# The long units of the second attention of an encoder layer: scores with keys on the partitions

## The reference

```python
def chunk_causal_attention(q, k, v):          # q, k: (B, H, S, 96), v: (B, H, S, 64)
    scale = dk ** -0.5
    for qb in range(S // 128):
        q0 = qb * 128
        L = q0 + 128
        s = einsum('bhqd,bhkd->bhqk', q[:, :, q0:L], k[:, :, :L]) * scale
        s = where(key // 64 <= query // 64, s, -inf)
        p = softmax(s)
        outs.append(einsum('bhqk,bhkd->bhqd', p, v[:, :, :L]))
```

## Time and profile before

| what | value |
|---|---|
| median of 3 runs | 1380.7 us (1379.72 to 1380.89) |
| the profiled execution | 1381.86 us, of which its span 1380.1 us |
| granted TensorE clock, mean | 0.991 |
| TensorE (PE) busy | 1321.9 us, 96% of the span |
| VectorE (DVE) busy | 834.0 us, 60% |
| ScalarE (ACT) busy | 740.3 us, 54% |
| GpSimd (POOL) busy | 161.2 us, 12% |

### The profile page before, as it was taken

The page is one execution under the profiler, slowest core; times in us unless marked ns, Lnnn a source line. Parts: engine busy times, 40 slices in busy tenths (PEclk is TensorE's granted clock), DMA queues, the critical chain, the costliest instruction groups (busy, mean ns, idle before and its releaser), DMA issues.

```text
span 1380.1 us, 21741 instructions
## 1 busy us (share of the span) xinstructions
PE 1321.9 (96%) x8200; PEld 993.1 (72%) x8200; DVE 834.0 (60%) x1639; ACT 740.3 (54%) x1422; POOL 161.2 (12%) x263
## 2 busy tenths in 40 slices
PE   6999999999999989999999999999989999999995
PEld 5888998844445744545887887888667878888884
DVE  5523125547667877675777433435746787787876
ACT  6421177456657766666334334333325677776765
POOL 1000000012240050000000000000035122221221
PEclk9999999999999999999999999999999999999998
DMA  6141113450000030102113010000667999999993
GB/s 239 22 172 46 66 62 122 183 201 17 1 1 1 2 122 22 40 32 92 46 46 138 19 43 31 31 31 31 239 232 222 328 356 340 343 345 332 360 340 108
DMA packets 89219, 186.47 MB, mean 135 GB/s; under 512 B 14094, under 2 KB 25266, under 8 KB 88370
## 3 DMA queue, kind: packets, MB, share of 16 engines
q1 hardware_dynamic: 80050, 166.11, 33.5%
q0 software_dynamic: 7008, 19.28, 5.7%
q10 hardware_dynamic: 2080, 0.01, 0.1%
HBM read 165.45 MB, written 25.56 MB: 138 GB/s over the span
## 4 chain that ended last, share of the span: by engine, by line
PE 83%; DVE 5%; ACT 4%; DMA 4%; issue 2%; POOL 1%; DVEq 0%; ACTq 0%; SPq 0%; POOLq 0%
PE psum L2504 31%; PE psum L2752 19%; PE psum L2647 7%; PE psum L2488 7%; PE psum L2670 5%; PE psum L2629 4%; PE psum L2481 4%; DMA up_stage<-in_w_up 3%; PE psum L2977 3%; PE psum L2986 1%; PE psum L2908 1%; DVE up_rest L1997 1%; PE psum L2964 1%; ACT arena L1448 1%; DVE arena L1874 0%
## 5 line engine op out<-in xcount | busy, mean ns | idle before, releaser
L1138 ACT ACTIVATE arena<-psum 128x512 f32<-128x512 f32 (+3 forms) x195 | 85.9, 494 | 84.9 <-PE psum L2670 47.4
L2647 PE MATMUL psum<-arena 64*128 64x512 f32 (+7 forms) x384 | 115.4, 519 | 8.3 <-ACT arena L1429 5.8
L1874 DVE TENSOR_TENSOR_SCAN arena<-arena,singles 128x768 f32<-128x768 f32 (+7 forms) x64 | 86.4, 1364 | 53.7 <-POOL arena L935 47.5
L2647 PEld LDWEIGHTS psum<-arena 64*128 64x128 f32 (+1 forms) x384 | 49.2, 190 | 75.6 <-issue 48.3
L2670 PEld LDWEIGHTS psum<-ident,arena 128*128 128x128 f32 x576 | 66.2, 144 | 51.6 <-ACT arena L1138 26.4
L2488 PE MATMUL psum<-arena 128*128 128x512 f32 (+2 forms) x280 | 93.8, 488 | 0.8 <-DVE arena L1855 0.8
L2670 PE MATMUL psum<-ident,arena 128*128 128x128 f32 x576 | 86.1, 287 | 8.4 <-DVE arena L1874 4.4
L2481 PE MATMUL psum<-ident,arena 128*128 128x128 f32 (+1 forms) x520 | 73.4, 278 | 17.8 <-ACT arena L1156 9.4
L1997 DVE TENSOR_TENSOR down_rest<-down_stage,down_high 128x1024 fp32r<-128x1024 f32 x60 | 71.4, 1220 | 26.8 <-ACT down_high L1471 26.8
L2481 PEld LDWEIGHTS psum<-ident,arena 128*128 128x128 f32 (+1 forms) x520 | 59.2, 139 | 33.8 <-issue 19.1
L2629 PE MATMUL psum<-arena 128*64 128x512 f32 (+3 forms) x384 | 83.4, 515 | 0.0
(11 more groups left out here) (565 smaller groups left out, 3395.9 us busy)
## 6 DMA issues: line engine op xcount, KB each, us to landing
gate_stage<-in_w_gate SPq DMA_DIRECT2D x16, 2048.0 KB
up_stage<-in_w_up SPq DMA_DIRECT2D x16, 2048.0 KB
down_stage<-in_w_down SPq DMA_DIRECT2D x15, 2048.0 KB
arena<-in_x SPq DMA_DIRECT2D x16, 512.0 KB, 3.9
arena<-in_w_mkv SPq DMA_DIRECT2D x8, 1024.0 KB, 6.2
arena<-in_w_in SPq DMA_DIRECT2D x4, 1024.0 KB, 10.9
arena<-in_w_mo SPq DMA_DIRECT2D x4, 1024.0 KB, 6.4
mv_times_w_mo_spill<-arena SPq DMA_DIRECT2D x8, 512.0 KB, 3.1
```

What stands on the lines that cost most here:

```text
L1138: do(act.activation(dst, src, ACT.Copy), s_te["act"])
L1874: do(dve.tensor_tensor_scan(w_row(u, r, a)[:, 0:L][:, ::-1], f_sb[:, n % FAILS, 0:L][:, ::-1], tiny.to_broadcast([P, L]), 1.0, ALU.mult, A ...
L2647: mm = pe.matmul(scores_of(kind, n)[:, at:end], lhs, rhs(at, end), start=True, stop=True)
```

## The change

The short units stay as they are. For a long unit:

- **Maximum pass.** ScalarE copies keys and queries of the next pair to float32r (`long_high`, 4 copies) and VectorE makes the rests (`long_rests`, 4 subtractions; for unit 4 GpSimd makes them). TensorE makes each row once, high by high only, in two products of half the row's width (`row_product`), always into banks 2 and 3. VectorE masks and takes the maximum (`row_maximum`). Row k waits for the maximum of row k - 1.
- **Shift inside the product.** The negative maxima are turned (`minus_maxima_turned`, 4 turns) and copied by ScalarE as rows 96 to 99 under the queries (`minus_maxima_copied`, 2 copies); the keys get matching rows of ones (`head_pick`). The product then gives score minus maximum.
- **Turned scores.** TensorE makes the scores again with keys on the partitions, block of 128 keys j by block, for both heads: two products each of the rests (`rest_products`) and one with the shift (`high_products`). ScalarE makes the exponentials of a block of both heads at once into `probs` (4 buffers), and writes zeros where the mask cuts (j of 4 and more). TensorE multiplies by the values (`value_products`).
- **Sums.** GpSimd adds the 8 blocks (7 additions of up to 2 x 512 columns a partition), TensorE sums over keys with a product of ones (`sums_over_keys`, bank 3), VectorE takes the reciprocal of 512 columns and multiplies (`long_out`).
- **Order.** The rows of unit u + 1 stand on TensorE at blocks 3 to 6 of unit u, two each; the first waits for `long_out(u - 1)`. The rows of unit 4 stand in unit 3, two at each block. Both late tiles are turned up in unit 1. The folded copies of the output projection's weights and the loads of the next weights wait for the new products.

```diff
+def of_block(i):
+    return PAIRS + i // ROWS, i % ROWS, P * max(0, i % ROWS - GRP)
+def added_through(i):
+    return (ROWS - 1) * (i // ROWS) + i % ROWS
...
-    return (("kf", "qf")[j], T - 2 if u == 1 else T - 1) if u in (1, PAIRS - 1) and j in (0, 1) else None
+    return (("kf", "qf")[j % 2], T - 2 + j // 2) if u == 1 else None
...
+        k_high = [over(f"mla_keys_high_{i}", F32R, at, 2, SEQ) for i, at in enumerate((36864, 41216))]
+        q_high = [[over(f"mla_queries_high_{i}{a}", F32R, at, GRP * P)[:, :] for a, at in enumerate(ats)]
+                  for i, ats in enumerate(((38912, 40704), (43264, 43776)))]
+        probs = [cut(44288 + 2 * GRP * P * i, 2, GRP * P) for i in range(4)]
+        prob_sums = [cut(at, 2, GRP * P) for at in (39424, 48384)]
+        one_over = cut(49408, GRP * P)
+        minus_max = over("minus_maxima", F32R, 16192, QK + 4 * GRP)[:, :]
+        maxima_of = cut(16304, 2 * GRP)
+        head_pick = cut(16312, 2)
+        ROWS_END = QK + 4
...
+        def turned_scores(i):
+            return psum[:, 4:6, :] if i % 2 == 0 else psum[:, 0:2, :]
+        def row_scores(k):
+            return psum[:, 2:4, 0:P * (GRP + k // 2 + 1) // 2]
+        def pieces(p):
+            late = slice(GRP * P, SEQ)
+            return ([(k_high[p % 2][0:QK, a, :], k_rest[0:QK, 2 * p + a, :], mkT_h[0:QK, 2 * p + a, :]) for a in range(2)]
+                    + [(q_high[p % 2][a][0:QK, :], q_rest[0:QK, 2 * p + a, late], mqT_h[0:QK, 2 * p + a, late]) for a in range(2)])
+        def pieces_through(p):
+            return HIGHS_BEFORE + 4 * (p + 1)
+        def maxima_ready(u, k=ROWS + 1):
+            return SHORT_ROWS + (ROWS + 1) * (u - PAIRS) + k
...
-                sp.wait_ge(s_ms, ROWS * (PAIRS + h // 2 + 1))
+                sp.wait_ge(s_sc, SB_ROWS + ROWS * (h // 2 + 1))
...
+            pool.wait_ge(s_ms, ROWS)
+            for i, (high, rest, raw) in enumerate(pieces(0)):
+                pool.wait_ge(s_kqh, HIGHS_BEFORE + i + 1)
+                pool.tensor_tensor(rest, raw, high.bitcast(F32), ALU.subtract).then_inc(s_kql, 1)
+            for i in range(LONG):
+                u, j, lo = of_block(i)
+                if j == 0:
+                    continue
+                total = prob_sums[u % 2]
+                pool.wait_ge(s_e, SHORT_ROWS + i + 1)
+                if j == 1:
+                    if u >= PAIRS + 2:
+                        pool.wait_ge(s_sum, SB_ROWS + u - PAIRS - 1)
+                    pool.tensor_tensor(total, probs[(i - 1) % 4], probs[i % 4], ALU.add).then_inc(s_add, 1)
+                else:
+                    pool.wait_ge(s_add, SB_ROWS + added_through(i - 1))
+                    pool.tensor_tensor(total[:, :, lo:], total[:, :, lo:], probs[i % 4][:, :, lo:], ALU.add).then_inc(s_add, 1)
...
+                        if kind == "mla" and u == 2 and j >= 0:
+                            long_high(0, j)
...
+            def long_high(p, i):
+                high, _, raw = pieces(p)[i]
+                if p == 0:
+                    act.wait_ge(s_hsum, 2)
+                if p >= 2:
+                    act.wait_ge(s_sc, SB_ROWS + ROWS * (p - 1))
+                act.wait_ge(s_te["act"], EMPTIED[ROUND["qf", T - 1, 1]][1])
+                act.activation(high, raw, ACT.Copy).then_inc(s_kqh, 1)
+            def minus_maxima_copied(u):
+                act.wait_ge(s_nt, TURNS_BEFORE + u - PAIRS + 1)
+                for a in range(2):
+                    act.activation(q_high[u % 2][a][QK:ROWS_END, :], bank(2)[QK:ROWS_END, :], ACT.Copy).then_inc(s_nr, 1)
+            def w_o_high(c):
+                if c == 0:
+                    act.wait_ge(s_wo, 16)
+                act.wait_ge(s_sc, SB_ROWS + ROWS * (c // 2 + 1))
+                do(act.activation(wo_split[0][:, c, :], wo_raw[:, c, :], ACT.Copy, scale=gmix[:, c:c + 1]), s_woh)
+            def turned_exps(i):
+                u, j, lo = of_block(i)
+                if j == 0:
+                    minus_maxima_copied(u)
+                act.wait_ge(s_sc, SB_ROWS + i + 1)
+                if i >= 4:
+                    act.wait_ge(s_mpv, prod_count("mla", PAIRS - 1) + 2 * (i - 3))
+                    act.wait_ge(s_add, SB_ROWS + added_through(i - 4 + ((i - 4) % ROWS == 0)))
+                dst = probs[i % 4]
+                exp = act.activation(dst[:, :, lo:], turned_scores(i)[:, :, lo:], ACT.Exp, scale=QK ** -0.5)
+                if j < GRP:
+                    exp.then_inc(s_e, 1)
+                else:
+                    do(exp)
+                    do.settle()
+                    act.activation(dst[64:P, :, lo:lo + 64], tiny[64:P, 0:1].unsqueeze(2).to_broadcast([64, 2, 64]),
+                                   ACT.Copy).then_inc(s_e, 1)
+                if u + 1 < N_UNITS and j < 2:
+                    for k in (2 * j, 2 * j + 1):
+                        long_high(u - PAIRS + 1, k)
+                if u > PAIRS and j in (3, 5):
+                    w_o_high(2 * (u - PAIRS - 1) + (j == 5))
+                if u == N_UNITS - 1 and j == 2:
+                    act.wait_ge(s_sc, SB_ROWS + ROWS * (PAIRS - 1))
+                    act.wait_ge(s_sum, SB_ROWS + PAIRS - 1)
+                    act.wait_ge(s_mo, PAIRS)
+                    mix_high_and_square(0)
...
+            for i in range(LONG):
+                u, j, lo = of_block(i)
...
+            def row_maximum(u, k):
+                src = row_scores(k)
+                h = src.shape[-1]
+                dve.wait_ge(s_ms, SHORT_ROWS + ROWS * (u - PAIRS) + k + 1)
+                one(dve.memset(src[0:64, 1, h - 64:h], -1e30))
+                dve.tensor_reduce(maxima_of[:, k:k + 1], src, AX.XY, ALU.max).then_inc(s_nb, 1)
+            def minus_maxima(u):
+                by_tile = maxima_of.rearrange("p (r a) -> p r a", a=2)
+                dst = minus_max[:, QK:].rearrange("p (r c a) -> p r c a", r=GRP, c=2)
+                dve.wait_ge(s_nb, maxima_ready(u, ROWS))
+                one(dve.tensor_scalar(dst[:, :, 0, :], by_tile, -1.0, None, ALU.mult))
+                dve.scalar_tensor_tensor(out=dst[:, :, 1, :], in0=by_tile, scalar=-1.0, in1=dst[:, :, 0, :].bitcast(F32),
+                                         op0=ALU.mult, op1=ALU.subtract).then_inc(s_nb, 1)
+            def long_rests(p):
+                for i, (high, rest_, raw) in enumerate(pieces(p)):
+                    dve.wait_ge(s_kqh, HIGHS_BEFORE + 4 * p + i + 1)
+                    dve.tensor_tensor(rest_, raw, high.bitcast(F32), ALU.subtract).then_inc(s_kql, 1)
+            def long_out(u):
+                p = u - PAIRS
+                dve.wait_ge(s_sum, SB_ROWS + p + 1)
+                one(dve.reciprocal(one_over, bank(3)))
+                dve.wait_ge(s_mpv, prod_count("mla", u))
+                do(dve.tensor_tensor(mixT[:, 4 + p, GRP * P:SEQ], bank(6 + u % 2), one_over, ALU.mult), s_mo)
+            do(dve.tensor_copy(minus_max[:, 0:QK], tiny[:, 0:1].to_broadcast([P, QK])))
+            do.settle()
+            for k in range(ROWS):
+                row_maximum(PAIRS, k)
+                if k == 1:
+                    out_rows("mla", 2, s_mpv, s_mo, 4)
+            minus_maxima(PAIRS)
+            out_rows("mla", 3, s_mpv, s_mo, 4)
+            for u in range(PAIRS, N_UNITS - 1):
+                long_rests(u - PAIRS + 1)
+                if u > PAIRS:
+                    long_out(u - 1)
+                for k in range(ROWS):
+                    row_maximum(u + 1, k)
+                minus_maxima(u + 1)
+                if u > PAIRS:
+                    w_o_rest(u - 1)
...
+                        if kind == "mla" and u == PAIRS - 1:
+                            for k in (2 * j, 2 * j + 1):
+                                row_product(PAIRS, k)
...
+            def row_product(u, k):
+                p, r, a = u - PAIRS, k // 2, k % 2
+                dst = row_scores(k)
+                h = dst.shape[-1]
+                if k == 0:
+                    pe.wait_ge(s_kqh, pieces_through(p))
+                    if u >= PAIRS + 2:
+                        pe.wait_ge(s_mo, u - 1)
+                    if u > PAIRS:
+                        pe.wait_ge(s_nr, SB_ROWS + 2 * p)
+                else:
+                    pe.wait_ge(s_nb, maxima_ready(u, k))
+                for part in range(2):
+                    mm = pe.matmul(dst[:, part, :], q_high[p % 2][a][0:QK, r * P:(r + 1) * P],
+                                   k_high[p % 2][0:QK, a, part * h:part * h + h], start=True, stop=True)
+                mm.then_inc(s_ms, 1)
...
+            def minus_maxima_turned(u):
+                pe.wait_ge(s_nb, maxima_ready(u))
+                for r in range(GRP):
+                    mm = pe.transpose(bank(2)[0:ROWS_END, r * P:(r + 1) * P], minus_max[:, 4 * r:4 * r + ROWS_END].bitcast(F32), ident[:, :])
+                mm.then_inc(s_nt, 1)
+            def rest_products(i):
+                u, j, lo = of_block(i)
+                p, cols = u - PAIRS, slice(j * P, (j + 1) * P)
```

(63 more changed lines are left out.)

142 lines of the change are left out of this document (58 added, 84 removed).

## The result

The change made the kernel slower: 1421.35 us in the median of 4 runs (1416.76 to 1426.6) against 1380.43 (1379.72 to 1380.89), a ratio of 1.0299 (95% interval 1.0282 to 1.0316). I had said 1392.7, at most 1402. The sign was right, the size was missed by 29 us, and the runs lie 10 us apart where those of before lie 1 us apart, which I had not expected at all.

What follows compares the result with a forecast made beforehand. TensorE, 96% busy, bounds the kernel; the changed maximum pass becomes a TensorE-VectorE loop. 2.0 + 18.7 + 24.6 + 2 x 29.3 + 18.7 = 122.6 against 114.3 us, with 4 for blocking +12.3: 1392.7 median, range 1380 to 1402.

Steps and rivals of the forecast that it cites:

- start of u3: Unit 3 starts 2 us later: more late heads turned in unit 1, ScalarE copies in unit 2, two rows saved.
- I leave it within the range: Granted clock: holes of 4 us before row 0 may lower it now and then, mostly hidden by VectorE's loops; not priced.
- GpSimd beside VectorE: GpSimd's additions and VectorE's rests block each other in three units: 1.3 us each, 4 in all, bounds 0 and 4.
- done before: Unit 3: GpSimd's four rests for unit 4 follow ScalarE's copies and are finished in time.
- rival (C): Blocking at its full 4 us a unit: 8 more than forecast, 1401 us; chance 0.13.
- Then the last GpSimd additions and the final sums, 1.6: End of the last unit: 1.6 us behind TensorE's 17.1, making 18.7 against 14.1.
- The reciprocal: VectorE's reciprocal of 512 columns in `long_out`, ahead of row 0: 4.4 us, bounds 0.7 and 4.4.
- Rival (B): Loop holds but the reciprocal is as quick as other operations: 1381.6 to 1385.5 us; chance 0.16 together with (D), same time.
- The loop: Maximum pass: each row waits for the previous row's reduction; 12.8 us for 7 turns, 17.4 from row 0 to next unit.
- Row 0 at 7.2 in unit 4, TensorE's 7.6 elsewhere: Row 0, from the unit's first high product: 7.2 us in unit 4; elsewhere 7.6 by TensorE, 11.8 to 11.9 by VectorE.
- The last unit without GpSimd: Last unit makes no rows: 17.1 us before the last GpSimd additions and final sums.
- Rival (A): Faster: TensorE stays the bound, reciprocal 0.7, loop hidden; units 22, 22, 21, 18, 13 us less, 1367; chance 0.10.

Runs made afterwards that it cites:

- run 9: Changed kernel with the edits of run 2, run 5, run 7 and run 8, and TensorE summing the last unit's blocks 6 and 7: 1385.13 us, ratio 1.0007.
- run 10: Run 9 with the row products one block earlier (blocks 2 to 5 in place of 3 to 6): 1387.12 us, ratio 1.003.
- run 5: Changed kernel with GpSimd's four rests for unit 4 waiting for the first row product of unit 3: 1423.49 us, ratio 1.0312.
- run 6: Changed kernel with 24 unread TensorE products of 512 columns ahead of row 0 in units 5 and 6: 1424.01 us, ratio 1.0322.
- run 7: Changed kernel with a separate reduction and signal for each of a row's two banks: 1413.88 us, ratio 1.0248.
- run 2: Changed kernel with GpSimd's additions waiting until VectorE's four rests for the next unit are done: 1408.21 us, ratio 1.0187.
- run 3: Changed kernel with all but one column per head of each GpSimd addition left out: 1406.44 us, ratio 1.0176.
- run 8: Run 2 with the sums copied by ScalarE and reciprocal and multiplication made after the row maxima: 1403.88 us, ratio 1.0186.
- run 11: Changed kernel with later quotient, reductions of 64 columns of either half and additions of one column per head: 1399.81 us, ratio 1.0128.

## Why the prediction was wrong

The working was right where it was a chain of VectorE's and TensorE's rows at full clock, and wrong in three steps that I priced low or not at all: the lower clock behind a hole, GpSimd beside VectorE, and the end of the last unit. Forecast and measured of the profiled executions:

```
                 start of u3   u3     u4     u5     u6     u7    
forecast            +2.0      18.7   24.6   29.3   29.3   18.7   (and 4.0 of blocking apart)
measured            +4.0      23.6   28.8   35.2   34.8   23.4
```

- **"I leave it within the range" (the granted clock): failed.** I had the earlier trace rows with 0.89 behind a hole of 2.6 us and knew of holes of 4 us to come, and still put their price at nothing, hidden by VectorE's loop. It isn't hidden: the value products and scores between the rows are on the path. By pairs of the same code at two clocks: unit 3 3.8 us (runs 9 and 10, so with half rows; no run has the changed kernel's unit 3 at a higher clock), unit 4 2.8 (row 0 at + 10.4, at + 7.5 to 7.8 in runs 5 to 7 where the clock had come back; the blocking would have taken the same time, see run 5, so this part belongs to both), units 5 and 6 2.0 and 1.5 (18.3 at full clock). Together 10 us. It is also part of what spreads the runs: unit 6 makes 2.4 of the 3.5 us between the two traced executions of the changed kernel. Over its eight executions the time rises as the mean clock falls, but loosely (1416.6 and 1422.32 us both at 0.974).
- **"GpSimd beside VectorE", 1.3 a unit: failed by size.** The first and second additions met both short rests: 5.52 in place of 1.38 (4.1 us in units 5 and 6 each, run 2); in unit 4 one met an addition, at no cost beside the low clock. I also left out two other meetings: GpSimd's rests with VectorE's scalings ahead of unit 3 (2.5 us, run 5), under "done before"; and in the last unit the additions with the weight and mix rests. The upper bound of 4 a unit was right for the rests, and rival (C) used it.
- **"Then the last GpSimd additions and the final sums, 1.6": failed.** The last unit is 4.4 us shorter without the additions (run 3), most of it TensorE's wait of 3.7. I asked whether TensorE's work was done, not whether GpSimd still kept up. Up to block 3 it did, at 2.4 us an addition. The last four took 9.21 us where, with nothing beside them and 0.14 between them, they would take 6.6. So 2.6 us of the wait is the blocking again, with the two engines' parts exchanged, and about 1.1 is the backlog that remains (an estimate from these numbers). With the point before, this makes 15 us, of which 4 were in the forecast.
- **The reciprocal: right kind, a fourth too dear.** 3.35 us, 6.2 ns for each column more than eight ((3350 - 203) / 504) and not 8.25. Two of them on the path: 2.2 us less than forecast. Rival (B), which had 0.7, is refuted.
- **The loop: right.** From row 0 to the next unit I had 17.4; at full clock it is 18.3. Over three units the missing 0.9 (the turns and the end of a unit) make 2.7 us.
- **Row 0 at 7.2 in unit 4, TensorE's 7.6 elsewhere: right**, where the clock is full and VectorE out of the way (7.2 to 8.3 in runs 8, 9 and 11).
- **The last unit without GpSimd: a little short.** Run 3 has 19.0. My 18.7 had the last additions in its 1.6; without them it was about 18.1 (17.1 and 1.0 for the sums).

Clock 10, blocking and the last addition 11 above the 4, reciprocal -2, loop 3: 22 of the 23 us by which the stretch exceeded the forecast. The pairs of the first point are from different executions and the attribution is good to a microsecond or two. The miss of the median is 29 and not 23, as I had set the median 1.2 us below the profiled execution and it lies 4.6 above it, the profiled one being the fastest of four; where the others lost these is in no trace. Rival (A) failed by its own terms too: run 11 gives it what it asks for, and TensorE still needs 23 us a unit and the stretch is 5.8 us shorter, not 13.

The Trainium skill (SBUF — State Buffer, "SBUF: two separate sides") says that a GpSimd operation and a VectorE operation with two SBUF inputs hold the shared ports for a whole instruction and the other waits. The rests agree: one took 676 ns, the median of the six 2772; the scalings of run 5, which read one tensor from SBUF, were lengthened too (1402 ns against 418). The Trainium skill's page names a second case there, an operation of VectorE in a two-port mode; that the scalings ran in one is shown by no run here.

What stays open: what decides whether the clock falls behind a given hole (run 6 and unit 3 of runs 9 and 10 show that it isn't the hole alone), and where the untraced runs lose it. What the clock costs is measured; that the holes bring it down rests on the holes standing ahead of each loss in units 5 and 6 and on the one filled unit that kept it.
